# A hybrid decoder trunk on one core: the convolution branch's projection and taps moved to the front of the mixer

## The reference, cut to what matters

```python
def hybrid_mixer(h, ...):
    proj = h @ w_in                      # gates | A: u, v | B: q, k, v | C: cq, ckv, kr | D: a, g
    o_a = chunked_sgu(u, v, ...)         # A: LayerNorm of v, 128x128 position mixing, times u
    o_b = moba_attention(qb, kb, v)      # B: block attention, QK norm, rotary; one block here
    o_c = mla_attention(cq, ckv, kr, ..) # C: latents -> norm -> up-projection -> QK norm -> attention
    o_d = conformer_conv(da, dg, ...)    # D: GLU, causal depthwise conv of width 31, LayerNorm, swish
    y = sum(sigmoid(gates[n]) * (o @ w_branch[n]) for n, o in enumerate((o_a, o_b, o_c, o_d)))
    return y @ w_out

def conformer_conv(a, g, conv_w, conv_b, ln_g, ln_b):
    z = a * jax.nn.sigmoid(g)
    z = lax.conv_general_dilated(z, conv_w[:, None, :], ...) + conv_b
    return jax.nn.silu(layernorm(z, ln_g, ln_b))
```

## Time and profile before

| | |
|---|---|
| median of 3 runs | 1142.72 us |
| the profiled execution: its own time | 1142.13 us |
| its span | 1140.4 us |
| mean granted TensorE clock | 0.978 |
| PE busy | 1078.8 us, 95% |
| DVE busy | 839.2 us, 74% |
| ACT busy | 646.6 us, 57% |
| mixer of layer 0, first to last matmul | 17.14 to 234.5 us |
| mixer of layer 1, first matmul | 448.80 us |

### The profile page before, as it was taken

How to read it: one execution, slowest core, us unless ns; L and a number is a source line. 1 busy time by engine, 2 the same in 40 slices (tenths; PEclk the granted TensorE clock), 3 DMA queues, 4 the chain that set the end, 5 groups by cost and what they waited for, 6 DMA issues and landing times.

```text
span 1140.4 us, 15778 instructions
## 1 busy us (share of the span) xinstructions
PE 1078.8 (95%) x5632; PEld 917.4 (80%) x5632; DVE 839.2 (74%) x1178; ACT 646.6 (57%) x904; POOL 29.0 (3%) x76
## 2 busy tenths in 40 slices
PE   5999899979999997999989979999999999999997
PEld 5888687879999996888777857788787878788886
DVE  4679888644445446479898664988888888889895
ACT  4666545443434335457545345666767676667763
POOL 6000000030000000000000000000000000000000
PEclk9999989999999998999999988999999999999999
DMA  9544445646455553454435474888898989898981
GB/s 270 166 166 153 142 133 203 209 134 204 166 184 172 174 184 120 157 167 143 153 129 183 135 272 138 298 317 316 304 338 287 356 281 355 283 357 285 347 293 47
DMA packets 125324, 248.64 MB, mean 218 GB/s; under 512 B 4912, under 2 KB 50034, under 8 KB 125280
## 3 DMA queue, kind: packets, MB, share of 16 engines
q1 hardware_dynamic: 123136, 243.02, 61.9%
q0 software_dynamic: 2144, 5.03, 1.8%
HBM read 246.99 MB, written 1.05 MB: 217 GB/s over the span
## 4 chain that ended last, share of the span: by engine, by line
PE 74%; DVE 18%; ACT 5%; issue 2%; DMA 1%; ACTq 0%; DVEq 0%; POOL 0%; POOLq 0%
PE bank L348 22%; PE bank L350 21%; PE bank L349 21%; DVE wlo L336 8%; ACT whi L329 3%; PE bank L894 2%; PE bank L893 2%; PE bank L953 1%; DVE dacc L1554 1%; DVE h L1349 1%; PE bank L914 1%; DVE x L1347 1%; PE bank L915 1%; DVE h L1486 1%; PE bank L611 1%
## 5 line engine op out<-in xcount | busy, mean ns | idle before, releaser
L336 DVE TENSOR_TENSOR wlo<-ring,whi 128x1024 fp32r<-128x1024 f32 (+3 forms) x506 | 541.5, 1122 | 111.8 <-ACT whi L329 110.9
L329 ACT CAST whi<-ring 128x1024 fp32r<-128x1024 f32 (+3 forms) x506 | 457.0, 972 | 30.1 <-PE bank L350 18.7
L348 PE MATMUL bank<-whi,hTh 128*128 128x256 f32 (+3 forms) x768 | 263.9, 344 | 5.4 <-DVE wlo L336 4.3
L349 PE MATMUL bank<-wlo,hTh 128*128 128x256 f32 (+3 forms) x768 | 259.1, 337 | 0.0
L350 PE MATMUL bank<-whi,hTl 128*128 128x256 f32 (+3 forms) x768 | 259.0, 337 | 0.0
L348 PEld LDWEIGHTS bank<-whi,hTh 128*128 128x128 f32 x768 | 148.4, 193 | 19.6 <-DVE hTl L1328 5.2
L349 PEld LDWEIGHTS bank<-wlo,hTh 128*128 128x128 f32 x768 | 148.5, 193 | 12.5 <-issue 0.5
L350 PEld LDWEIGHTS bank<-whi,hTl 128*128 128x128 f32 x768 | 148.3, 193 | 12.7
L348 PE MATMUL bank<-whi,xgh 128*128 128x512 f32 (+1 forms) x384 | 149.5, 389 | 5.6 <-DVE wlo L336 2.9
L349 PE MATMUL bank<-wlo,xgh 128*128 128x512 f32 (+1 forms) x384 | 145.2, 378 | 0.0
L350 PE MATMUL bank<-whi,xgl 128*128 128x512 f32 (+1 forms) x384 | 145.1, 378 | 0.0
(11 more groups left out here) (305 smaller groups left out, 1113.7 us busy)
## 6 DMA issues: line engine op xcount, KB each, us to landing
ring<-in_w_in SPq DMA_DIRECT2D x40, 1024.0 KB, 5.2
ring<-in_moe_w_down SPq DMA_DIRECT2D x40, 1024.0 KB, 5.8
ring<-in_moe_w_gate SPq DMA_DIRECT2D x32, 1024.0 KB, 7.8
ring<-in_moe_w_up SPq DMA_DIRECT2D x32, 1024.0 KB, 7.5
ring<-in_moe_w_gate SPq DMA_DIRECT2D x16, 768.0 KB, 5.6
ring<-in_moe_w_up SPq DMA_DIRECT2D x16, 768.0 KB, 4.5
ring<-in_ffn_w_gate SPq DMA_DIRECT2D x11, 1024.0 KB, 5.2
ring<-in_ffn_w_up SPq DMA_DIRECT2D x11, 1024.0 KB, 5.2
```

Source lines behind the costliest of these rows:

```text
L329: nc.scalar.copy(whi[pc.part(hf)][:, 0:n], pc.raw[:, hf * n:(hf + 1) * n]).then_inc(hi_done, 1)
L336: nc.vector.tensor_tensor(wlo[q][:, 0:n], pc.raw[:, hf * n:(hf + 1) * n], whi[q][:, 0:n].bitcast(F32), ALU.subtract).then_inc(lo_done, 1)
L348: nc.tensor.matmul(o, sh, wh, start=start, stop=False)
L349: nc.tensor.matmul(o, sh, wl, start=False, stop=False)
```

## The change

The D chunk goes to the front of `CHUNKS`, so all other chunks come two pieces later. D's chain (eviction with sigmoid, `glu`, `d_zT`, copy to `zpad`) is put at s = 1 and 2, and the taps start at s = 3: 18 of the 62 are now done by s = 7, where before none was done ahead of s = 13. Of the taps between the block attention's scores and its `probs_T`, 4 are left (`taps[19]`, put ahead of `softmax_end`), where 12 stood before (`taps[17]` and `taps[19]`). The work of C and A is shifted back by one to two pieces each (`c_latent_T` 3 to 5, `c_up` 4 to 6, `a_z` 6 to 7, `c_qkT` 9 to 10, `scores(0)` 10 to 11); `a_oT` stays at s = 8. D's mean and centring move from s = 26 to 24, `d_finish` from 28 to 26, its last subtraction from 29 to 28.

```diff
-CHUNKS = [(C_Q, 352), (A_U, 512), (B_Q, 384), (B_Q + 384, 384), (D_A, 512)]
+CHUNKS = [(D_A, 512), (C_Q, 352), (A_U, 512), (B_Q, 384), (B_Q + 384, 384)]
...
             def d_zT(l):
+                pe.wait_ge(hT_lo, 8 * l + 4)
                 pe.wait_ge(glu_ready, l + 1)
-                pe.wait_ge(sc_ev, 8 * l + 4)
...
                 def small(s):            # PE
                     if s == 2:
+                        d_zT(l)
                         prep(l)
-                    if s == 3:
+                    if s == 5:
                         c_latent_T(l)
-                    if s == 4:
+                    if s == 6:
                         c_up(l)
-                    if s == 6:
+                    if s == 7:
                         a_z(l)
                     if s == 8:
                         a_oT(l)
...
                     if s == 1:           # ACT
                         chunk_ev(0)
+                    if s == 2:
+                        act_e.wait_ge(zT_mm, l + 1)
+                        nc.scalar.copy(zpad[:, :, D_CONV - 1:D_CONV - 1 + T],
+                                       bank[5][:, :].rearrange("p (c t) -> p c t", t=T)).then_inc(zpad_ready, 1)
+                    if s == 3:
+                        chunk_ev(1)
                         square_latents()
...
-                taps = {13: (0, 8), 14: (8, 4), 16: (12, 6), 17: (18, 2), 19: (20, 10), 20: (30, 8), 22: (38, 10),
-                        23: (48, 10), 25: (58, 4)}
+                taps = {3: (0, 4), 4: (4, 2), 5: (6, 10), 7: (16, 2), 13: (18, 5), 14: (23, 5), 16: (28, 7), 19: (35, 4),
+                        20: (39, 3), 22: (42, 10), 23: (52, 10)}
...
                     if s == 2:           # DVE
-                        c_norm_latents(l)
+                        glu(l)
                         prep(l)
...
                     if s == 19:
+                        conv_taps(l, *taps[s])
                         softmax_end(l, 1, 0)
```

More of the change, by code:

```diff
@@ L631, in d_zT @@
             def d_zT(l):
+                pe.wait_ge(hT_lo, 8 * l + 4)
                 pe.wait_ge(glu_ready, l + 1)
-                pe.wait_ge(sc_ev, 8 * l + 4)
                 for c in range(2):
                     for m in range(MT):
-                        last = nc.tensor.transpose(bank[6][:, T * c + P * m:T * c + P * (m + 1)],
+                        last = nc.tensor.transpose(bank[5][:, T * c + P * m:T * c + P * (m + 1)],
                                                    dxc[:, m, P * c:P * (c + 1)], ident[:, :])
@@ L750, in small @@
                         a_oT(l)
-                    if s == 9:
+                    if s == 10:
                         c_qkT(l)
-                    if s == 10:
+                    if s == 11:
                         scores(l, 0)
-                    if s == 11:
-                        d_zT(l)
+                    if s == 13:
                         b_qkT(l)
@@ L1136, in mixer @@
                         up_evict()
-                    if s == 5:
-                        chunk_ev(2)
+                    if s == 7:
+                        chunk_ev(3)
                         act_e.wait_ge(qms, l + 1)
@@ L1141, in mixer @@
                                              scale=1.0 / C_QK).then_inc(qms_root, 1)
-                    if s == 7:
-                        chunk_ev(3)
                     if s == 8:
-                        act_e.wait_ge(prj_ev, n_chunk * l + 4)
-                        nc.scalar.activation(ym[:, :, 0:512], prj[:, :, B_Q:B_Q + 512], ACT.Square).then_inc(b_sq, 1)
                         o_upper(l, 0, 6)
                     if s == 9:
+                        chunk_ev(4)
+                        act_e.wait_ge(prj_ev, n_chunk * l + 5)
+                        nc.scalar.activation(ym[:, :, 0:512], prj[:, :, B_Q:B_Q + 512], ACT.Square).then_inc(b_sq, 1)
+                    if s == 10:
                         act_e.wait_ge(bms, l + 1)
@@ L1160, in mixer @@
                         gate_ev(0)
-                        act_e.wait_ge(zT_mm, l + 1)
-                        nc.scalar.copy(zpad[:, :, D_CONV - 1:D_CONV - 1 + T],
-                                       bank[6][:, :].rearrange("p (c t) -> p c t", t=T)).then_inc(zpad_ready, 1)
+                    if s == 12:
+                        attention_exp(l, 0, 0)
+                    if s == 13:
+                        attention_exp(l, 0, 1)
                         act_e.wait_ge(sc_mm, 8 * l + 4)
@@ L1616, in mixer @@
                     if s == 2:
-                        c_norm_latents(l)
+                        glu(l)
                         prep(l)
                     if s == 4:
+                        c_norm_latents(l)
+                    if s == 6:
                         a_norm(l)
-                    if s == 5:
+                    if s == 7:
                         c_sum_qk(l)
-                    if s == 6:
+                    if s == 8:
+                        a_gate(l)
                         c_scale_qk(l)
-                    if s == 7:
-                        a_gate(l)
+                    if s == 9:
                         c_rotate_qk(l)
-                    if s == 8:
                         o_lower(l, 0, 6)
-                    if s == 9:
+                    if s == 10:
                         b_sum_qk(l)
-                    if s == 10:
                         b_rotate_qk(l)
-                        glu(l)
+                    if s == 11:
                         softmax_start(l, 0)
@@ L1651, in mixer @@
                         merge(l, merges[s], pcs[s])
-                    if s in taps:
+                    if s in taps and s != 19:
                         conv_taps(l, *taps[s])
+                    if s == 24:
+                        d_center(l)
                     if s == 26:
-                        d_center(l)
+                        d_finish(l)
                     if s == 28:
-                        d_finish(l)
-                    if s == 29:
                         dve.wait_ge(o_hi[3], l + 1)
```

35 lines of the change are left out of this document (16 added, 19 removed).

## The result

| | before | after |
|---|---|---|
| median | 1141.36 us | 1146.41 us |
| lowest to highest | 1139.70 to 1143.18 us | 1142.92 to 1148.34 us |
| runs | 11 | 11 |
| the profiled execution | 1142.13 us | 1148.34 us |
| its span | 1140.4 us | 1146.6 us |

The changed kernel is slower: the ratio on record is 1.0037, with an interval of 1.0027 to 1.0048, so 4.2 us; the two medians alone are 5.05 us apart. The profiled execution of after is the highest of its runs, 1.9 us above their median. One execution of the kernel before, timed beside the last two experiments, took 1775.12 us at a mean granted clock of 0.556 and is left out of all numbers here.

What follows compares the result with a forecast made beforehand. PE, busy 95% of the span, was the bound. Idle 5.3 us more, less 4.3 of old slow clock, plus 6.0 of new, gave 1149.1 for the profiled execution; forecast 1149.5 us, range 1142.0 to 1154.0.

Steps and rivals of the forecast that it cites:

- Idle at D's transposes: Transposes of D's input at s = 2, waiting for the GLU product: PE idles 3.2 us per layer.
- A's transposes: Transposes of A's output at s = 8, waiting for A's gate on DVE: PE idles 3.0 us per layer.
- Probabilities: Block attention's probabilities at s = 20: eight taps leave the chain, 1.1 us of 4.3 stays, slow clock goes.
- The mean: Convolution's mean at s = 24, waiting for the last taps: PE idles 1.4 us per layer.
- The tail: Late mixer: the 1.99 us wait for D's result goes; gate piece 28 waits for its sigmoid, taken as 0.9 us.
- Layer 0 alone: Layer 0's larger first piece: PE starts 0.3 us later, first idle grows 0.7; 1.0 us in all.
- The clock: Behind four long waits at D's and A's transposes, both layers: three slow stretches at 2.0 us, 6.0 us.
- the clock holds: Rival: none or one of the four idle times lowers the clock; 1143.7 to 1145.7 us; chance 0.18.
- Faster: Rival: DVE paces PE no more from s = 19, 3.4 us a layer; 1136.9 us or no change; chance 0.10.
- Not what it says: Rival: something other than taps holds the probabilities, idle stays near 4.3 us with slow clock; 1160 us; chance 0.04.
- More than forecast: Rival: all four idle times lower the clock, 4 x 2.4 us, or early waits longer; 1153 to 1156 us; chance 0.13.

Runs made afterwards that it cites:

- the last two experiments: Kernel with later D transposes, A's gate moved ahead of piece 10's remainders: 1134.97 us; then that kernel with C's scaling earlier and taps spread anew: 1124.05 us.
- the second experiment: Changed kernel plus unread products on PE, 10 ahead of D's transposes and 9 ahead of A's: 1142.09 us, ratio 1.0002.
- The third experiment: Changed kernel with the 7 taps of s = 16 moved between scores and probabilities, 11 there instead of 4: 1154.80 us, ratio 1.0111.
- The last experiment: Kernel with later D transposes and earlier A's gate, plus C's scaling at s = 7 and taps dealt out anew: 1124.05 us, ratio 0.9847.
- the first experiment: Changed kernel with D's transposes and the copy into zpad one piece later (s = 3), first taps at s = 4: 1136.19 us, ratio 0.995.

## Why the prediction was right

The direction and the mechanisms held; the time was 3.1 us lower than forecast, within the range. The direction hung on the clock. Without the new slow stretches the terms nearly cancel, as the prediction's own sum had it (1.0 us slower), and the second experiment shows it: ratio 1.0002.

- **Idle at D's transposes**, forecast 3.2 us: 3.22 in both layers.
- **A's transposes**, 3.0: 2.73 and 2.72. The sum was long by 0.3.
- **Probabilities**, 1.1 and a full clock: 1.12, clock 1.00. The third experiment repeats the price per tap.
- **The mean**, 1.4: 1.32.
- **The tail**, between 0 and 1.99, taken as 0.9: 0.58, and released by the gate sigmoid as described. The wait of branch piece 30, C's query transposes and the scores: none, as forecast.
- **Layer 0 alone**, 1.0 us, out of 0.3 and 0.7: PE started 0.93 us later (18.07 against 17.14). The larger piece accounts for 0.33 of it, as forecast: the wait in front of PE's first product is 3.58 us, and 3.25 before. The other 0.6, which nothing in the prediction stands for, was the landing of the norm's gain, which let DVE's first row start at 10.00 and not at 9.41 in this execution. The 0.7 for the late weights of piece 3 did not come: ACT had them in time, and the first idle is 3.22 and not 3.9. That the total fits is luck.
- **The clock**, four long waits, three slow stretches at 2.0 us: the profiled execution has four at about 1.7. For the median the second experiment gives 4.3 us in place of 6.0. This is the term that was mis-sized the most. Its size in the profile was close to the forecast's per stretch; how many stretches a run has was taken by judgement.

The sum for the profiled execution: 2 x (8.97 - 7.45) = 3.0 us of idle, 0.9 of start, 4 x 1.7 = 6.8 of new slow clock less 4.3 of old. That is 6.4 us; measured, 1148.34 - 1142.13 = 6.2. For the median, three terms pull the same way: the clock's part by 1.7 us, the idle and the start by 1.3 (3.0 + 0.9 against 5.3), and the reference by 1.4, since the kernel before has its median at 1141.36 us over 11 runs and not at 1142.72 as over the three. That is 4.4 us for the 3.1 missed; the other 1.3 has no term. The loss itself is known no better than to about a microsecond: 4.2 us by the ratio, 5.05 by the medians. Two sums in the prediction are off on paper: 1149.1 plus 0.6 is 1149.7 and not 1149.5, and the chances that it adds to 0.75 make 0.78. Neither changes the verdict.

Of the rivals, "the clock holds" is refuted for the profiled execution, but its time, 1143.7 to 1145.7, holds one of the 11 runs, three more lie below it, and its upper end is 0.7 us from the median. "Faster", by which DVE would pace PE no more from s = 19 on, did not happen: all three waits of the late stage are there, with DVE or ACT behind it as releaser. The last experiment shows what it takes: 3 taps instead of 10 ahead of the mean, more of them placed early, and both DVE waits are gone.

"Not what it says" is refuted by the 1.12 us in front of the probabilities and by the third experiment. "More than forecast" had the profiled execution right in the number of stretches, four, and wrong in their size, 1.7 and not 2.4 us.

One thing in the working was too simple. It put the threshold for a slow stretch between 1.99 and 4.3 us of idle, as if the length decided alone. The runs show 1.95, 1.93, 2.34 and 2.33 us with a slow stretch behind them, 1.99 without, and 2.72 to 2.75 four times with and twice without.

## What to carry to other kernels

Moving a chain to the front of a pipeline pays only if enough work lies between its parts there to cover it. Count for each hand-over what the waiting engine still has to do against the length of the chain, and move the consumer one slot later where that comes out short: here one slot was worth 10 us. Moving A's gate one slot ahead won only 1.2 us, since the wait came back at the next product that needed the same engine. Try the parts of a change apart, as the smaller part (which table row holds a dozen small instructions) may be the whole gain. And a wait of 2 to 4 us on TensorE may cost another 1.4 to 3.0 us behind it in clock, so that filling it with useless products can pay where it can't be removed.

## What the runs showed of the hardware

- The length of an idle time does not alone say whether the clock falls. Behind 1.99 us it stayed at the full 2.4 GHz (in the kernel before, 512-column products of the branch behind it). Behind 1.95 and 1.93 us it was at 1.2 GHz for most of 3.5 to 4.0 us (16 transposes of 128 columns behind it). Behind 2.34 and 2.33 us it was so for most of 4 us, with 512-column products behind it. Behind 2.72 us it was so in one layer and not in the other, in one execution (the first experiment), and in another behind 2.74 us and not behind 2.75 (the third). What decides is left open. Most of these stretches cost 1.7 us, the time at half clock times the share of the clock that is missing.
- A slow stretch can come without a long wait in front of it. At the start of layer 1's mixer PE waits 0.63, 0.67 and 0.55 us with four transposes between, the same in every kernel here, and the clock has been full for some 6 us before them; behind them it is 0.51 in after and 1.00 in the first experiment. It costs some 1.6 us where it comes, whatever was changed, and so belongs in any account of two single executions.
- "TensorE: Matmul & The Clock Gate" of the Trainium skill, section "What's actually happening", says that the number of slow matmuls at a kernel's start varies between runs of one kernel. No kernel here was profiled twice; what agrees with it is that the mean granted clock of the 11 runs of after lies between 0.975 and 0.983. The rows above are of stretches in mid-kernel, and in them a stretch may be missing altogether.
- The same first transfers of a launch land at different times. These are the casts of the second piece, which wait for its landing, in after and in the first two experiments (whose transfers are the same):

```profile
18.28 1.99 ACT L329 CAST whi<-ring 128x1024 fp32r<-128x1024 f32 x2 [1.04 <-DMA ring<-in_w_in]
```

```profile
19.90 1.99 ACT L329 CAST whi<-ring 128x1024 fp32r<-128x1024 f32 x2 [2.32 <-DMA ring<-in_w_in]
```

```profile
21.56 1.99 ACT L329 CAST whi<-ring 128x1024 fp32r<-128x1024 f32 x2 [4.34 <-DMA ring<-in_w_in]
```

  They differ by 3.3 us. In the last of them D's transposes of layer 0 came 2.0 us later than in after (39.89 against 37.90) and their idle was 1.61 us where layer 1 had 0.94. So up to 2 us of such a spread can be in the time of a single run.
